# Stick-breaking attention: the query blocks of a pair from the widest to the narrowest

## What is computed

```python
def stick_breaking_attention(q, k, v):
    """q, k, v: (B, H, S, dh). A[t,s] = beta[t,s] * prod_{s<j<t} (1 - beta[t,j]), s < t."""
    seq = q.shape[2]
    scale = 1.0 / math.sqrt(q.shape[-1])
    outs = []
    for t0 in range(0, seq, Q_BLOCK):
        t1 = t0 + Q_BLOCK
        z = jnp.einsum('bhqd,bhkd->bhqk', q[:, :, t0:t1], k[:, :, :t1]).astype(jnp.float32) * scale
        causal = jnp.arange(t1)[None, :] < (t0 + jnp.arange(Q_BLOCK))[:, None]
        log_stay = jnp.where(causal, jax.nn.log_sigmoid(-z), 0.0)
        log_between = lax.cumsum(log_stay, axis=3, reverse=True) - log_stay
        weights = jnp.where(causal, jnp.exp(jax.nn.log_sigmoid(z) + log_between), 0.0)
        outs.append(jnp.einsum('bhqk,bhkd->bhqd', weights.astype(v.dtype), v[:, :, :t1]))
    return jnp.concatenate(outs, axis=2)

def stick_breaking_mixer(h, w_qkv, q_gain, k_gain, w_o):
    ...
    q, k, v = jnp.split(h @ w_qkv, 3, axis=-1)
    q = rmsnorm(q.reshape(bsz, seq, SB_HEADS, SB_HEAD_DIM), q_gain)
    k = rmsnorm(k.reshape(bsz, seq, SB_HEADS, SB_HEAD_DIM), k_gain)
    ...
```

## Time and profile before

| | |
|---|---|
| median of 3 runs | 2741.28 us (2739.74 to 2741.86) |
| the profiled execution | 2739.28 us, span 2737.6 us |
| its PE, DVE, ACT, POOL busy | 96%, 60%, 27%, 17% of the span |
| mean granted clock of TensorE | 0.982 |
| stick-breaking pairs, 1410 to 1648 us | 238 us |

### The profile page before, as it was taken

One profiled execution on the slowest core, in us unless ns is written; L12 is line 12 of the kernel. 1 busy time (PEld: TensorE's weight loads), 2 busy tenths in 40 slices (PEclk: granted clock), 3 DMA queues, 4 the chain that ended last, 5 costly groups with the idle time before them and its releaser, 6 DMA issues.

```text
span 2737.6 us, 38434 instructions
## 1 busy us (share of the span) xinstructions
PE 2617.0 (96%) x12249; PEld 2058.1 (75%) x12249; DVE 1653.0 (60%) x2625; ACT 745.1 (27%) x1386; POOL 459.5 (17%) x458
## 2 busy tenths in 40 slices
PE   6999899999799989999989989999999999999999
PEld 4676688888567668888856657888888887788887
DVE  6765566454675566646467775644558888564452
ACT  2333232120233323212045552100024555210000
POOL 4111121112111111111211101111111110111111
PEclk8999999999899999999999999999999999999999
DMA  3221233332222123333311112333332211233333
GB/s 93 62 58 51 62 100 96 96 100 85 63 55 62 48 72 96 99 96 96 92 54 54 54 39 85 94 98 97 95 99 63 62 54 54 70 99 93 100 97 96
DMA packets 417268, 214.76 MB, mean 78 GB/s; under 512 B 6820, under 2 KB 416015, under 8 KB 417167
## 3 DMA queue, kind: packets, MB, share of 16 engines
q1 hardware_dynamic: 416144, 212.89, 26.9%
q10 hardware_dynamic: 1022, 0.58, 0.1%
HBM read 211.34 MB, written 2.10 MB: 78 GB/s over the span
## 4 chain that ended last, share of the span: by engine, by line
PE 82%; DVE 8%; ACT 4%; issue 4%; DVEq 0%; DMA 0%; POOL 0%; SPq 0%; ACTq 0%; POOLq 0%
PE acc L618 72%; PE sc L720 2%; PE sc L1016 2%; DVE xT L1308 1%; PE tp L739 1%; PE po L762 1%; ACT h_hi L1679 1%; ACT scratch L1836 1%; DVE scratch L1381 1%; PE tp L874 1%; ACT scratch L1834 1%; DVE w_lo L1181 0%; PE po L1039 0%; DVE scratch L1248 0%; DVE scratch L1375 0%
## 5 line engine op out<-in xcount | busy, mean ns | idle before, releaser
L618 PE MATMUL acc<-h_hi,w_hi 128*128 128x512 f32 x2048 | 846.3, 413 | 49.5 <-DVE h_lo L1111 30.6
L618 PE MATMUL acc<-h_hi,w_lo 128*128 128x512 f32 x2048 | 805.1, 393 | 0.0
L618 PE MATMUL acc<-h_lo,w_hi 128*128 128x512 f32 x2048 | 803.8, 392 | 0.0
L571 POOL TENSOR_SCALAR w_hi<-w_raw 128x1024 fp32r<-128x1024 f32 x398 | 422.4, 1061 | 2255.7 <-PE acc L618 2255.7
L1181 DVE TENSOR_TENSOR w_lo<-w_raw,w_hi 128x1024 fp32r<-128x1024 f32 x398 | 484.9, 1219 | 70.2 <-POOL w_hi L571 69.7
L618 PEld LDWEIGHTS acc<-h_hi,w_hi 128*128 128x128 f32 x2048 | 387.7, 189 | 182.7 <-DVE h_lo L1111 48.3
L618 PEld LDWEIGHTS acc<-h_hi,w_lo 128*128 128x128 f32 x2048 | 387.4, 189 | 84.4
L618 PE MATMUL acc<-mid_hi,w_hi 128*128 128x512 f32 x1120 | 441.9, 395 | 6.6 <-DVE mid_lo L1639 3.2
L618 PEld LDWEIGHTS acc<-h_lo,w_hi 128*128 128x128 f32 x2048 | 388.8, 190 | 78.2 <-issue 6.7
L618 PE MATMUL acc<-mid_lo,w_hi 128*128 128x512 f32 x1120 | 440.4, 393 | 0.0
L618 PE MATMUL acc<-mid_hi,w_lo 128*128 128x512 f32 x1120 | 439.5, 392 | 0.0
(11 more groups left out here) (288 smaller groups left out, 2513.3 us busy)
## 6 DMA issues: line engine op xcount, KB each, us to landing
w_raw<-in_mlp_w_dram SPq DMA_DIRECT2D x128, 512.0 KB, 4.0
w_raw<-in_w_in_dram SPq DMA_DIRECT2D x48, 512.0 KB, 3.8
w_raw<-in_w_gate_dram SPq DMA_DIRECT2D x44, 512.0 KB, 3.7
w_raw<-in_w_up_dram SPq DMA_DIRECT2D x44, 512.0 KB, 3.7
w_raw<-in_w_down_dram SPq DMA_DIRECT2D x32, 512.0 KB, 4.0
w_raw<-in_hg_w_in_dram SPq DMA_DIRECT2D x32, 512.0 KB, 4.0
w_raw<-in_sb_w_qkv_dram SPq DMA_DIRECT2D x24, 512.0 KB, 3.7
w_raw<-in_w_out_dram SPq DMA_DIRECT2D x16, 512.0 KB, 4.0
```

The lines of the kernel that those rows point to most:

```text
L571: nc.gpsimd.tensor_scalar(w_hi[:, slot], w_raw[:, slot], 1.0, 1.0, ALU.mult, ALU.mult).then_inc(w_rounded, 1)
L618: mm = pe.matmul(bank[:], w[:, k], r[:, k], start=(k == 0 and i == 0), stop=(k == k_tiles - 1 and i == 2))
```

## The change

The step t of a pair takes query block NB - 1 - t in place of block t (NB = 4): the widths of steps 0 to 3 are 4, 3, 2 and 1 blocks in place of 1, 2, 3 and 4. The buffers of even and odd steps change places, since the even ones are now the larger. The transposes of the values on TensorE and their copy on ScalarE stand in slot 4 in place of slot 2.

```diff
--- before.py
+++ after.py
@@ -253,8 +253,8 @@
 
             return part(at, 2 * (t + 1) * P).rearrange("p (m c) -> p m c", m=2)
 
-        sb_soft = [two_heads(t, (4096, 4864)[t % 2]) for t in range(NB)]
-        sb_sum = [two_heads(t, (5888, 6656)[t % 2]) for t in range(NB)]
+        sb_soft = [two_heads(NB - 1 - t, (4864, 4096)[t % 2]) for t in range(NB)]
+        sb_sum = [two_heads(NB - 1 - t, (6656, 5888)[t % 2]) for t in range(NB)]
         sqT = [part(7936 + 512 * i, 512) for i in range(2)]
         skT = [part(8960 + 512 * i, 512) for i in range(2)]
 
@@ -863,7 +863,8 @@
 
                 def scores(t):
 
-                    step, n = 4 * p + t, (t + 1) * P
+                    step, b = 4 * p + t, NB - 1 - t
+                    n = (b + 1) * P
                     if t == 0:
                         pe.wait_ge(sb_qk_ready, 2 * p + 2)
                     if previous or t >= 2:
@@ -871,7 +872,7 @@
                         pe.wait_ge(w_ready, step - 1)
                     for m in range(2):
                         r = slice(HD * m, HD * m + HD)
-                        pe.matmul(z_pair[t % 2][:, m, 0:n], sqT[par % 2][r, t * P:t * P + P], skT[par % 2][r, 0:n],
+                        pe.matmul(z_pair[t % 2][:, m, 0:n], sqT[par % 2][r, b * P:b * P + P], skT[par % 2][r, 0:n],
                                   start=True, stop=True).then_inc(z_done, 1)
 
                 for k in range(SLOTS):
@@ -883,7 +884,7 @@
                         scores(t)
                     if current and k % 3 == 2 and (previous or t >= 2):
                         weighted(p if t >= 2 else p - 1, (par if t >= 2 else par - 1) % 2, behind)
-                    if current and k == 2:
+                    if current and k == 4:
                         pe.wait_ge(aux_free, aux_n)
                         u = 3 * par + 2
                         pe.wait_ge(evacuated[u % 2], U_SB // 2 + 3 * pp + u // 2 + 1)
@@ -900,7 +901,7 @@
 
                 pe.wait_ge(logw_done, 4 * p_ + t + 1)
                 for m in range(2):
-                    for j in range(t + 1):
+                    for j in range(NB - t):
                         mm = pe.transpose(z_pair[t % 2][:, m, j * P:j * P + P], sb_sum[t][:, m, j * P:j * P + P], ident[:])
                 mm.then_inc(wt_done, 1)
 
@@ -910,11 +911,12 @@
                     pe.wait_ge(aux_free, A_SB + 3 + 3 * p_ + 1)
                     pe.wait_ge(sb_o_taken, p_ + 1)
                 pe.wait_ge(w_ready, 4 * p_ + t + 1)
-                for j in range(t + 1):
+                b = NB - 1 - t
+                for j in range(NB - t):
                     for m in range(2):
                         r = slice(HD * m, HD * m + HD)
-                        mm = pe.matmul(po[r, t * P:t * P + P], sb_vtok[par_][:, j, r], sb_weights[:, m, j * P:j * P + P],
-                                       start=(j == 0), stop=(j == t))
+                        mm = pe.matmul(po[r, b * P:b * P + P], sb_vtok[par_][:, j, r], sb_weights[:, m, j * P:j * P + P],
+                                       start=(j == 0), stop=(j == NB - 1 - t))
                 if t == NB - 1:
                     mm.then_inc(sb_pv_done, 1)
 
@@ -1369,7 +1371,7 @@
 
                 def log_weights(t):
 
-                    n = (t + 1) * P
+                    n = (NB - t) * P
                     v.wait_ge(z_log, 4 * p + t + 1)
                     soft, total, z = sb_soft[t], sb_sum[t], z_pair[t % 2][:, :, 0:n]
                     steps(STT(soft, z, 0.0, soft, ALU.max, ALU.add))
@@ -1831,7 +1833,7 @@
 
                     soft = sb_soft[t]
                     a.wait_ge(z_done, 2 * (4 * p + t) + 2)
-                    steps(ACTV(soft, z_pair[t % 2][:, :, 0:(t + 1) * P], ACT.Abs))
+                    steps(ACTV(soft, z_pair[t % 2][:, :, 0:(NB - t) * P], ACT.Abs))
                     steps.wait()
                     steps(ACTV(soft, soft, ACT.Exp, scale=-1.0))
                     steps.wait()
```

## The result

The changed kernel takes 2750.94 us (median of 20 runs, 2742.46 to 2754.74); the kernel before, run beside it, 2739.9 us (2737.31 to 2741.86). The ratio is 1.0035, with a 95% interval of 1.0029 to 1.0041. The forecast was 2738.4 us with a range up to 2745.5, and 0.12 for "slower by over 0.2%". The scatter itself has changed: 12 us after, 4.5 us before.

A forecast was written before the change was run, and what follows sets the result against it. TensorE, busy 96% of the span, was taken as the bound, so only its stalls or lower clock could be won. Pair 0 +1.4, pairs 1 to 6 +4.6, last pair -8.9: 2741.28 - 2.9 = 2738.4 us, range 2732.5 to 2745.5.

The forecast's parts named there:

- The wait for the values goes: TensorE's wait of 0.8 us a pair for the values' copy out of PSUM falls to zero.
- The wait for the exponential grows: TensorE's stall before scores(3), behind VectorE's and ScalarE's queues, grows from 0.5 to 1.8 us a pair.
- GpSimd in the way: GpSimd's rounding delays the two scans of log_weights(0) on VectorE by 0.3 us a pair, bounds 0 and 1.05.
- The last pair: From pair 7's first scores to the first product needing its result: 26.8 us against 35.66, so -8.9.
- Pair 0: From its first scores to pair 1's: +1.4 us, including about 0.35 of waiting for log_weights(0).
- The clock: TensorE's clock was taken as full in the pairs; only its half speed after the last stall, 3.40 us, was kept.
- The sum of -2.9 us: The whole change in time: +1.4 at the first pair, +4.6 over pairs 1 to 6, -8.9 in the last.
- the likeliest case: The time stays within 0.2% (5.5 us) of before, with up to three clock falls; chance 0.60.
- Rival B: TensorE's clock falls behind the grown stall, 1.6 us each; six falls give 2748 us; over +0.2%, chance 0.12.
- a granted clock under 1.00 in the pairs: Sign of being wrong: TensorE's granted clock under 1.00 between 1435 and 1615 us of the profile.

The follow-up runs named there:

- e2: The kernel before with only the transposes of the values and their copy moved to slot 4, block order unchanged: 2739.43 us, ratio 0.9996.
- e3: The changed kernel with VectorE's sb_take (result of the pair before) moved in front of log_weights(1): 2727.54 us, ratio 0.9951.
- e5: The changed kernel with ScalarE's sb_high moved behind softplus(2), sb_take left in place: 2731.53 us, ratio 0.9965.
- e7: The kernel before with the values' transposes in slot 4 and the widths reversed in the last pair alone: 2732.67 us, ratio 0.9965.
- e9: The changed kernel itself run again for a second profile: 2751.67 us, ratio 1.0040.
- e4: The changed kernel with two unused products of constants added on TensorE in front of scores(3): 2743.99 us, ratio 1.0020.
- e1: The changed kernel with the transposes of the values and their copy put back to slot 2: 2752.44 us, ratio 1.0042.
- e10: The changed kernel with sb_take in front of log_weights(1) and sb_high behind softplus(2): 2726.35 us, ratio 0.9949.
- e8: The changed kernel with one unused product of constants added on TensorE in front of scores(3): 2744.96 us, ratio 1.0017.
- e6: The changed kernel with a second, unused GpSimd operation of the same size ahead of the rounding L571 in the pairs' units: 2748.66 us, ratio 1.0030.

## Why the prediction was wrong

- **The wait for the values goes: right.** It is gone in each pair. But e2 shows that it was worth 1.9 us over six pairs and not 4.6, since the chain before scores(3) stood right behind it.
- **The wait for the exponential grows: right in its mechanism.** The chain was forecast at 22.9 us without GpSimd, and measured 23.86 with 0.80 from the scans; e3 and e5 show that both queues named are in it.
- **GpSimd in the way: a term that was mis-sized.** I took 0.3 us between the bounds 0 and 1.05; it is 0.8. The nearer row was an operation that met GpSimd in its second half; the second scan starts 0.7 us after GpSimd's operation, which itself was stretched, and still meets most of it. Over six pairs the 0.5 us missing are 3.0 us. The Trainium skill ("VectorE: DVE Perf Modes", section "Two Vector instructions with no wait between them") has the second SBUF input read through an interface shared with GpSimd. The trace agrees: the period of 31.0 us that the prediction had worked out by that rule is nearer to the measured 30.89 than my 30.25.
- **The last pair: right,** -8.8 against -8.9, and by its mechanism: counted from the first scores, log_weights(0) starts at 4.41 (forecast 4.44) and sb_take at 13.81 (13.82). Of the gain, 6.8 us are separable (e7).
- **Pair 0: +2.2 against +1.4,** mostly since TensorE waited 0.94 us there for log_weights(0), not 0.35:

```profile
1419.15 1.09 PE L905 MATMUL sc<-ident,scratch 128*128 128x128 f32 x8 [0.94 <-DVE scratch L1386]
```

- **The clock: the step that failed.** The sum of -2.9 us holds nothing for falls in the pairs; the likeliest case allowed three at most, and over +0.2% was a rival of 0.12. Without falls the terms measured give +2.2 + 8.2 - 8.8 = +1.6 us, inside the range. With the larger stall, 2.8 us and not 2.1, an execution has up to six falls, and six cost 10.5 us: 195.10 us for pairs 1 to 6 in e9, against 184.58 in e4, where the same period holds none. Rival B named the mechanism, the place and the price (1.6 us each; measured 1.4 to 1.7 in most pairs), and a granted clock under 1.00 in the pairs was among the prediction's own signs of being wrong. My chance for it was wrong for two reasons. First, I did not carry GpSimd's upper bound into it: at 1.05 the stall is 2.8, beyond the longest that had kept its clock, 2.30; the two terms were treated as separate though one decides the other. Second, I set one stall with a fall behind it (2.18) against one without (2.30), and the last pair of the same profile has two more, both with a fall:

```profile
1617.51 1.09 PE L891 MATMUL aux<-ident,yT 128*128 128x128 f32 x4 [2.94 <-DVE yT L1402]
1631.58 2.08 PE L874 MATMUL tp<-scratch 64*128 64x512 f32 x4 [2.29 <-ACT yT L1870]
```

```profile
1617.51:1620.51 3.00, 3.00 (x13) 2.71 (x13) 2.90 (x6) 0.77 (x2) 0.00 (x0) 0.50 0.18 47
1631.58:1635.58 4.00, 4.00 (x8) 1.66 (x8) 3.64 (x5) 1.82 (x2) 0.00 (x0) 0.50 0.00 0
```

Of four stalls of 2.2 to 2.9 us three were followed by the lower clock, which was no ground for 0.12. The Trainium skill ("TensorE: Matmul & The Clock Gate", section "HAM oscillation — how this bites in real kernels") says that a wait recurring in each turn of a loop can drop the clock in each turn; e1 and e9 agree with it, with a fall in each of six pairs.
- **Slips in the working, none of which decides.** Steps 0 and 1 of log_weights grow by 9.38 - 5.14 = 4.2 us, not 5.3. GpSimd at its bounds changes six periods, which makes -4.7 and +1.6 us, not -4.9 and +2.1. Five falls make -2.9 + 8.0 = +5.1 us, still under the 5.5 of 0.2%: rival B decides from the sixth fall.

**Open:** why one execution has two falls and another six at the same stall. No run was made that could place them.

## What to carry to other kernels

Reversing an order changes which short instruction stands behind which long one. Follow each queue to the instruction that was cheap to wait for, here a copy of 0.68 us; moving that one copy turned +0.4% into -0.5% (e3, 2727.5 us; e10, with both moves, 2726.4).
A stall on TensorE in a loop has two prices: its own length, and that of the clock's fall behind it. When a chain's uncertainty could carry the stall past what the profile has shown to be tolerated, count both in one case, and times the number of turns. Before giving that case a chance, read the granted clock behind every stall of that length in the profile, not behind one or two.

## What the runs showed of the hardware

- The clock of TensorE stayed at full with stalls of about 1.0 us in each pair (e4, e5), fell in one pair of six at 1.9 us (e8), and in two to six of six at 2.6 to 2.8 us (the changed kernel, e1, e6, e9). It fell behind three of four stalls of 2.2 to 2.9 us in the last pair of the kernel before. A fall cost 1.4 to 1.7 us in most pairs and 2.9 in the first of e1 and e9. Filling the stall with products that nobody needs kept the clock up in all six pairs of the profile (e4).
- An operation of VectorE with two inputs in SBUF and one of GpSimd (L571) held each other back: scan 1.2 to 2.0 us, subtraction 0.69 to 1.59, GpSimd 1.05 to 1.6 or 1.7. In the overlaps shown the later one was stretched, and VectorE's where both began together (e6, 1521.29).
